# In the last dense head, one of three PSUM copies of the transposed probabilities goes from ScalarE to VectorE

## What is computed

```python
s = jnp.einsum('bqhcd,bkhcd->bhcqk', q_blk, k).astype(jnp.float32) * scale
p = jax.nn.softmax(s, axis=-1)
a = p[:, :, 0] - lam * p[:, :, 1]
return jnp.einsum('bhqk,bkhv->bqhv', a.astype(v.dtype), v)
```

## Time and profile before

| | us |
|---|---|
| median of 3 runs | 1846.29 |
| the profiled execution | 1846.72 |
| its span (first to last instruction) | 1845.4 |
| PE busy | 1695.6 (92%) |
| DVE busy | 1104.9 (60%) |
| ACT busy | 886.8 (48%) |
| POOL busy | 403.8 (22%) |

### The profile page before, as it was taken

How to read it: one execution, slowest core, us unless ns; L and a number is a source line. 1 busy time by engine, 2 the same in 40 slices (tenths; PEclk the granted TensorE clock), 3 DMA queues, 4 the chain that set the end, 5 groups by cost and what they waited for, 6 DMA issues and landing times.

```text
span 1845.4 us, 35790 instructions
## 1 busy us (share of the span) xinstructions
PE 1695.6 (92%) x13754; PEld 1579.1 (86%) x13754; DVE 1104.9 (60%) x2535; ACT 886.8 (48%) x2652; POOL 403.8 (22%) x390
## 2 busy tenths in 40 slices
PE   3898999999999999888999989999999999998896
PEld 2888898999998888767999988989999988886796
DVE  6476485335547676875155754853355476787627
ACT  4444544435526575774045335344355165676603
POOL 5331131120031011120454311311301111022044
PEclk9899999999999898999999999999999999999998
DMA  7110110110030101143112101001101201113312
GB/s 262 48 47 12 47 36 24 59 47 10 10 98 21 39 24 45 25 145 101 47 69 94 35 13 58 25 24 58 47 10 33 83 15 46 39 33 131 123 47 92
DMA packets 97849, 102.44 MB, mean 56 GB/s; under 512 B 7504, under 2 KB 87616, under 8 KB 97424
## 3 DMA queue, kind: packets, MB, share of 16 engines
q1 hardware_dynamic: 96720, 99.08, 16.7%
q10 hardware_dynamic: 960, 1.07, 0.2%
HBM read 70.43 MB, written 21.17 MB: 50 GB/s over the span
## 4 chain that ended last, share of the span: by engine, by line
PE 71%; DVE 15%; ACT 7%; POOL 3%; issue 2%; DMA 2%; SPq 0%; ACTq 0%; DVEq 0%
PE psum L881 45%; PE psum L1021 6%; PE psum L956 4%; PE psum L1075 3%; ACT p_b L1479 3%; PE psum L1176 3%; PE psum L1160 3%; DVE p_b L1967 2%; DVE row_max L1953 2%; PE psum L1061 1%; POOL w_lo L846 1%; PE psum L928 1%; ACT aT_b L1489 1%; PE psum L1004 1%; PE psum L999 1%
## 5 line engine op out<-in xcount | busy, mean ns | idle before, releaser
L881 PE MATMUL psum<-w_hi,hT_hi 128*128 128x256 f32 x1824 | 528.0, 289 | 6.0 <-POOL w_lo L846 4.2
L881 PE MATMUL psum<-w_hi,hT_lo 128*128 128x256 f32 x1824 | 516.0, 283 | 0.0
L881 PE MATMUL psum<-w_lo,hT_hi 128*128 128x256 f32 x1824 | 515.8, 283 | 0.0
L842 POOL CAST w_hi<-w_raw 128x512 fp32r<-128x512 f32 (+1 forms) x168 | 108.1, 643 | 1294.0 <-DMA w_raw<-in_w_in 715.7
L881 PEld LDWEIGHTS psum<-w_hi,hT_hi 128*128 128x128 f32 x1824 | 346.8, 190 | 14.2 <-POOL w_lo L846 5.1
L881 PEld LDWEIGHTS psum<-w_hi,hT_lo 128*128 128x128 f32 x1824 | 346.7, 190 | 0.0
L881 PEld LDWEIGHTS psum<-w_lo,hT_hi 128*128 128x128 f32 x1824 | 346.6, 190 | 0.0
L881 PE MATMUL psum<-hT_hi,w_hi 128*128 128x346 f32 (+1 forms) x672 | 230.7, 343 | 9.4 <-DVE hT_lo L1603 9.4
L881 PE MATMUL psum<-hT_hi,w_lo 128*128 128x346 f32 (+1 forms) x672 | 221.4, 330 | 0.0
L881 PE MATMUL psum<-hT_lo,w_hi 128*128 128x346 f32 (+1 forms) x672 | 220.8, 328 | 0.0
L846 POOL TENSOR_TENSOR w_lo<-w_raw,w_hi 128x512 fp32r<-128x512 f32 (+1 forms) x168 | 213.5, 1271 | 27.0 <-DVE neg_max L1954 15.1
(11 more groups left out here) (164 smaller groups left out, 2619.7 us busy)
## 6 DMA issues: line engine op xcount, KB each, us to landing
w_raw<-in_w_in SPq DMA_DIRECT2D x72, 256.0 KB, 3.7
w_raw<-in_w_in SPq DMA_DIRECT2D x28, 512.0 KB, 4.4
h_dram<-hbuf SPq DMA_DIRECT2D x16, 512.0 KB, 2.6
w_raw<-in_w_out SPq DMA_DIRECT2D x16, 512.0 KB, 4.1
hbuf<-h_dram SPq DMA_DIRECT2D x16, 512.0 KB, 5.8
qk_b<-y_dram SPq DMA_DIRECT2D x16, 512.0 KB, 3.3
y_dram<-y_stage SPq DMA_DIRECT2D x96, 64.0 KB, 1.6
qk_t<-rot SPq DMA_DIRECT2D x56, 86.5 KB, 2.2
```

What stands on the lines that cost most here:

```text
L842: pool.tensor_copy(hi, raw).then_inc(w_hi_done, 1)
L881: last = nc.tensor.matmul(out_ap, lhs[a](k), rhs[b](k), start=k == 0 and a + b == 0, stop=k == KT - 1 and b == 1)
```

## The change

`evac_probs(t, 2)` leaves ScalarE's stream in the pass of the last head (it stays there in the passes of B0 to B2). VectorE gets a copy of the same 128x384 block, to the same place and with the same waits and release, after the second maximum and before the rest of the step. There are 9 such copies in layer 0 (the one of tile 8 has 3x16 columns) and 8 in layer 1.

```diff
                 if after:
                     exps(after, 0)
-                evac_probs(t, 2)
+                if nx:
+                    evac_probs(t, 2)
...
+            def evac_last(t):
+
+                key = ("aT", l, g, t, 2)
+                b, m = bank(key), rows(t)
+                wait_filled(dve, key)
+                wait_filled(dve, ("o", l, *b_step(l, g, t, -1)))
+                nc.vector.tensor_copy(aT_b[:, 6:9, 0:m],
+                                      psum[:, b, 0:3 * P].rearrange("p (k c) -> p k c", k=3)[:, :, 0:m])\
+                    .then_inc(released[b], 1)
...
                 if after:
                     maximum(after, 0)
                     maximum(after, 1)
+                if not nx:
+                    evac_last(t)
                 for j in before:
                     qk_lo(l, nx, j)
```

## The result

| | before | after |
|---|---|---|
| median of 12 runs, us | 1846.30 | 1852.82 |
| lowest and highest, us | 1842.75, 1854.55 | 1848.62, 1858.77 |
| profiled execution (span), us | 1846.72 (1845.4) | 1852.79 (1851.5) |
| ACT busy, DVE busy, us | 886.8, 1104.9 | 881.9, 1111.4 |

The ratio is 1.0034 (1.002 to 1.0049): +6.3 us (3.7 to 9.0). I had forecast +3.56, with 1851.2 as the upper end. So "slower by more than 0.2%", on which I put 0.44, came, and the time lies above the range.

A forecast was written before the change was run, and what follows sets the result against it. In the B3 passes two loops through the small engines were taken to bound the kernel, loop two without ScalarE. -0.64 + 1.96 + 1.47 + 0.68 + 0.09 = +3.56 us gave a median of 1849.8, range 1847.6 to 1851.2.

The forecast's parts named there:

- Loop one: Steps 0 to 3 of each B3 pass, 6.83 us a turn; in steps 1 to 3 the second bound leaves gain 0.00.
- Rival 2: ScalarE's order sets the time: 15 steps each give back 0.36 us, 5.4 faster, 1840.9; chance 0.04.
- rival 3: Steps 1 to 3: the bound comes earlier without waiting for GpSimd, but loop two holds; +1.4, 1847.7; chance 0.08.
- Step 0: First step of each B3 pass: without ScalarE's copy the second exponential begins 0.32 us sooner; both layers together -0.64.
- The copy hidden in loop one: Steps 0 to 3: VectorE idles 1.17 us before combine, so a copy of some 0.5 us counts 0.
- Rival 4: VectorE's copy isn't hidden in loop one either, with GpSimd blocking or 1 us copies: +10, 1856; chance 0.04.
- The price of a copy: Delay of what is queued behind one VectorE copy out of PSUM: 0.49 us, bounds 0.28 and 0.60.
- Rival 1: The copy reads two columns a cycle, distance 0.28: +1.9, 1848.2; chance 0.09.
- Loop two: From step 4 on, 7.40 us a turn without ScalarE; the copy adds 0.49 a step, 1.96 and 1.47 by layer.
- The last step: End of each B3 pass: finish and low part wait behind the copy; last values +0.68 in layer 1, +0.09 in layer 0.

The follow-up runs named there:

- second_bound: first_four, with GpSimd's low half (L846) in the B3 pass held until the second bound instead of the first; median 1845.02 us, ratio 0.9994 to the kernel before.
- the two free kernels: before_free and first_four_free: kernel before and first_four, with GpSimd's splitting of the second output weight chunk not held beside the maxima; ratios 1.0056 and 1.0043.
- first_four: Kernel before, but VectorE copies part 2 in steps 0 to 3 of the B3 passes only; median 1848.46 us, ratio 0.9994.
- copy_twice: Kernel after, but VectorE makes every copy of part 2 twice, except in the last steps; median 1861.3 us, ratio 1.0075 to the kernel before.
- last_only: Kernel before, but VectorE copies part 2 in the last step of each B3 pass only; median 1847.57 us, ratio 1.0.
- filler: Kernel after, plus twelve unread transposes in TensorE's longer idle time of each last step; median 1850.95 us, ratio 1.0014 to the kernel before.
- loop_two_only: Kernel before, but VectorE copies part 2 only from step 4 on, without the last step; median 1853.1 us, ratio 1.0028.
- all_but_last: Kernel after, but ScalarE makes the copy of part 2 again in the last step of each pass; median 1856.54 us, ratio 1.0043 to the kernel before.
- before_filler: Kernel before, plus the same twelve unread transposes as filler in the last step of each pass; median 1848.62 us, ratio 0.9994.
- before_free: Kernel before, with GpSimd's splitting of the second output weight chunk no longer held beside the maxima of the B3 pass; median 1859.59 us, ratio 1.0056.

## Why the prediction was wrong, and where it was right

- **Loop one, gain 0 in steps 1 to 3.** Right. The turn is 6.82, ScalarE waits 0.36 for the bound, and second_bound and the two free kernels show the cause: with GpSimd moved, the bound takes 0.16 and the copy's move gives 0.37 a turn. Rival 2 (ScalarE's order sets the time, faster) and rival 3 fall with it.
- **Step 0, -0.32 each.** Right: -0.31 from bound to exponential in layer 0, and in layer 1 the turn to the next scores is 6.41 instead of 6.74; first_four agrees in sign.
- **The copy hidden in loop one.** Right, with 0.21 us of TensorE's idle time left. Rival 4 falls for one copy, and copy_twice shows its edge.
- **The price of a copy, 0.49.** 0.47 in the trace, so 7 x 0.02 too much. Rival 1 (two columns a cycle, 0.28) falls.
- **Loop two, +0.49 a step.** Right: 7.86 where I had 7.89.
- **The last step, +0.68 and +0.09.** This is the step that failed: measured +1.65 in layer 1 and +1.58 in layer 0. Its queues were nearly right, +0.65 and +0.18 by last_only and filler. But I took each duration of TensorE from rows at full clock (the 1.83 us from the low part to the last values above all) and put a change of the clock at nothing, without a reason; the profile has it at 1.40 + 1.00 = 2.40 us. 1852.82 - 2.40 = 1850.42 would have been inside the range.

So the sum of the queues was right: +3.56 forecast, 1.55 + 1.09 + 0.18 + 0.65 = +3.47 in the traces, +3.5 (0.7) at equal clock. In the traces it is right term by term. In whole times it is partly luck: first_four has -1.3 (0.7) for the -0.64 of loop one, loop_two_only +4.5 (0.7) for the +3.4 of loop two, and the two misses cancel. What the sum lacked is the clock: 2.40 us in the profile. Over the runs, the kernel after and its repeat have a mean clock of 0.9687 (20 runs) and the kernel before 0.9707 (79 runs, standard deviation 0.0023). That is 0.0020 lower, some 2.7 us at 1.36 us for each 0.001 (1.3 to 4.2 with the scatter of both means), and 3.5 + 2.7 = 6.2. That this comes near the 6.3 measured is no second proof, since the fit splits the difference of the times into just these two parts. What ties the lower clock to the last step is filler: filling one idle time took it away in both layers of its profile, and the mean clock of its runs is back. It is one profile and twelve runs, and whether all of the 0.0020 falls in the last steps isn't shown: all_but_last has a lower mean clock still, 0.9674 over eight runs, and in its profile only one last step is low.

What sets off the low clock is less sure. Five profiles have the 1.48 us in one piece in layer 0, and all five are low there. Of the seven others without filler, with 0.96 to 1.09, three are low (second_bound and the two free ones) and four aren't. In layer 1 two of five with 1.38 are low, and two of seven with less. That is seven of ten last steps with the long idle time and five of fourteen without it, and none of filler's and before_filler's four. So the long idle time may make it likelier, which these counts alone don't prove, and it isn't needed: before_free has the idle times of the kernel before (0.99 and 0.97, 1.03 and 0.88) and is low in both. In each kernel but the kernel after it is one execution, and why loop_two_only's mean clock is 0.9702 with the same idle times stays open.

## What to carry to other kernels

Moving work off an engine named by the chain gains nothing where the other input of the next instruction comes at the same moment: compare the two ends, and look for what delays the later one (here GpSimd beside a 128x1 instruction). Price the move in each loop by what bounds that loop, since the same copy is free in one and paid whole in the other; and then look at TensorE's idle times, because their pattern can change while their sum stays, and a clock that falls behind them stretches durations that the old profile shows at full clock: here 2.4 us beside 3.5 of queues. One profile can't tell such a cost from luck; the mean clock of many executions can.

## What the hardware showed that I hadn't expected

- A TensorE at the lower clock for 3 to 4 us costs 1.40 us in layer 0 and 1.00 in layer 1 (last steps of 7.63 and 7.96 against filler's 6.23 and 6.96). The mean clock of executions of one kernel varies by itself with a standard deviation of 0.0023, some 3 us of time.
- A VectorE copy out of PSUM keeps its length when GpSimd's L846 starts in the middle of it (0.56 us in second_bound, and 0.56 in loop two without GpSimd), while a 128x1 instruction with SBUF operands waits for its end (1.04 instead of 0.15). The Trainium skill (SBUF — State Buffer, "Who interferes with whom") says that only a VectorE instruction with two SBUF inputs, or in a mode with both ports, contends with GpSimd; the trace of second_bound agrees. It doesn't test a copy that starts behind L846 and lies wholly beside it. So a copy out of PSUM is a good candidate to put beside GpSimd's work.
